# A streaming encoder step: the feed-forward in two phases, with the gate and up projections by a seven-product scheme

## The reference

```python
def causal_dwconv(u, prev, w, b):
    L = u.shape[1]
    full = jnp.concatenate([prev.astype(u.dtype), u], axis=1)
    out = b + sum(full[:, i:i + L] * w[i] for i in range(CONV_W))
    return out, full[:, -(CONV_W - 1):]

def conv_glu(h, prev, w_in, conv_w, conv_b, w_out):
    g, u = jnp.split(h @ w_in, [D_FF], axis=-1)
    gc, new_prev = causal_dwconv(g, prev, conv_w, conv_b)
    return (jax.nn.gelu(gc, approximate=False) * u) @ w_out, new_prev
```

## Time and profile before

| | before |
|---|---|
| median of 3 runs | 2745.13 us |
| profiled execution, first to last instruction | 2742.7 us |
| around that span, if it took the median | 2.4 us |
| TensorE busy | 2688.9 us (98%) |
| VectorE busy | 1199.6 us (44%) |
| ScalarE busy | 902.6 us (33%) |
| GpSimd busy | 799.4 us (29%) |
| DMA | 156.83 MB, mean 57 GB/s |

### The profile page before, as it was taken

The page is one execution under the profiler, slowest core; times in us unless marked ns, Lnnn a source line. Parts: engine busy times, 40 slices in busy tenths (PEclk is TensorE's granted clock), DMA queues, the critical chain, the costliest instruction groups (busy, mean ns, idle before and its releaser), DMA issues.

```text
span 2742.7 us, 41556 instructions
## 1 busy us (share of the span) xinstructions
PE 2688.9 (98%) x17198; PEld 2600.8 (95%) x17198; DVE 1199.6 (44%) x2298; ACT 902.6 (33%) x1617; POOL 799.4 (29%) x452
## 2 busy tenths in 40 slices
PE   8999999999999999999999989999999999999999
PEld 7899999999999999999998988888999999999999
DVE  6634344463333333333625866555633333333324
ACT  7333242451111111112447756444521111111121
POOL 4122221262222222223422223322532222222221
PEclk9999999999999999999999999999999999999999
DMA  3110101011111111111213352212011111111112
GB/s 106 37 39 30 49 20 49 21 46 47 47 47 47 47 47 47 47 47 47 68 43 121 110 215 95 83 53 70 16 47 47 47 47 47 47 47 47 47 47 80
DMA packets 156508, 156.83 MB, mean 57 GB/s; under 512 B 15121, under 2 KB 137631, under 8 KB 156207
## 3 DMA queue, kind: packets, MB, share of 16 engines
q1 hardware_dynamic: 153935, 152.20, 17.5%
q10 hardware_dynamic: 2400, 2.10, 0.3%
HBM read 128.12 MB, written 26.15 MB: 56 GB/s over the span
## 4 chain that ended last, share of the span: by engine, by line
PE 88%; DVE 6%; issue 2%; ACT 2%; DMA 1%; SPq 0%; POOL 0%; DVEq 0%; ACTq 0%; POOLq 0%
PE ps L309 25%; PE ps L310 24%; PE ps L311 24%; PE ps L1933 2%; PE ps L862 1%; PE ps L1917 1%; DVE xT L536 1%; PE ps L849 1%; PE ps L850 1%; PE ps L851 1%; DVE fa L721 1%; PE ps L933 1%; PE ps L918 1%; PE ps L1900 1%; PE ps L1899 1%
## 5 line engine op out<-in xcount | busy, mean ns | idle before, releaser
L309 PE MATMUL ps<-hh,whi 128*128 128x352 f32 x2664 | 864.6, 325 | 0.7 <-DVE hl L443 0.4
L310 PE MATMUL ps<-hl,whi 128*128 128x352 f32 x2664 | 854.8, 321 | 0.0
L311 PE MATMUL ps<-hh,wlo 128*128 128x352 f32 x2664 | 854.5, 321 | 0.0
L274 POOL TENSOR_TENSOR wlo<-wraw,whi 128x2048 fp32r<-128x2048 f32 (+1 forms) x79 | 361.6, 4577 | 652.5 <-ACT whi L267 623.0
L309 PEld LDWEIGHTS ps<-hh,whi 128*128 128x128 f32 x2664 | 500.6, 188 | 3.8 <-issue 1.3
L310 PEld LDWEIGHTS ps<-hl,whi 128*128 128x128 f32 x2664 | 501.4, 188 | 1.1 <-issue 0.2
L311 PEld LDWEIGHTS ps<-hh,wlo 128*128 128x128 f32 x2664 | 499.9, 188 | 0.0
L536 DVE TENSOR_TENSOR xT<-xT,ps 128x352 f32<-128x352 f32 x720 | 372.0, 520 | 262.7 <-PE ps L311 261.4
L267 ACT ACTIVATE whi<-wraw 128x2048 fp32r<-128x2048 f32 x82 | 157.1, 1915 | 578.6 <-DMA wraw<-w_ffn_in 456.7
L309 PE MATMUL ps<-fahi,whi 128*128 128x352 f32 x1056 | 343.5, 325 | 2.5
L311 PE MATMUL ps<-fahi,wlo 128*128 128x352 f32 x1056 | 341.2, 323 | 0.0
(11 more groups left out here) (330 smaller groups left out, 4223.1 us busy)
## 6 DMA issues: line engine op xcount, KB each, us to landing
wraw<-w_ffn_in SPq DMA_DIRECT2D x88, 512.0 KB, 5.0
wraw<-w_ffn_out SPq DMA_DIRECT2D x44, 512.0 KB, 3.9
wraw<-w_gla_in SPq DMA_DIRECT2D x24, 512.0 KB, 4.7
s_k<-kw SPq DMA_DIRECT2D x8, 784.0 KB, 3.3
akraw<-s_k SPq DMA_DIRECT2D x8, 784.0 KB, 4.3
s_v<-vst SPq DMA_DIRECT2D x8, 768.0 KB, 4.3
av<-s_v SPq DMA_DIRECT2D x8, 768.0 KB, 4.1
aqraw<-s_q SPq DMA_DIRECT2D x8, 528.0 KB, 5.7
```

Source lines behind the costliest of these rows:

```text
L274: pool.tensor_tensor(lo[:, 0:cols], raw[:, 0:cols], hi[:, 0:cols].bitcast(F32), ALU.subtract).then_inc(S("w_lo"), 1)
L309: nc.tensor.matmul(out, w[0], x[0], start=start, stop=False)
L310: nc.tensor.matmul(out, w[0], x[1], start=False, stop=False)
L311: return nc.tensor.matmul(out, w[1], x[0], start=False, stop=stop)
```

## The change

The feed-forward of each layer is cut into two phases. Phase one computes all gate and up tiles, phase two all down projections.

Tile f = 0 is computed as before. For the other 21 tiles the pair (gate, up) is one block product: the weights are a 2 x 2 block matrix (gate or up x k 0 to 3 or k 4 to 7), h is a 2 x 2 block matrix (k 0 to 3 or k 4 to 7 x the first or the last 528 tokens). Seven block products take the place of eight. `product` does one in 24 matmuls of 264 columns, into two PSUM banks. Three of the seven need sums of weights (S2, S3, S4, and a fourth in place of the gate-side block), four need sums of activations (T1 to T4, made once a layer in `t_sums`). ScalarE takes partial sums out of PSUM after products 1, 3 and 5 (`snap`), VectorE adds the other products to them (`gate_left`, `the_rest`).

h stays in SBUF as before; its sums T1 to T4 take the room of x and of the activations. So x goes to DRAM (`s_x`) before phase one and comes back at its end, and the hidden activations go to DRAM tile by tile (`s_a`) and come back in phase two, two at a time. VectorE's first operation of the feed-forward waits until x is out (`x_spilled`). The down projection is the same count of matmuls of 352 columns; the first group adds to the x that came back. The loops of SyncE, ScalarE, VectorE and GpSimd over groups are written out.

```diff
@@ -51,9 +51,11 @@
 FF = 2816
 NF = FF // P
 NFG = NF // 2
-NPAIR = (NFG - 1) // 2 - 1
-GW = 2 + SEQ + 2 + DEC
-CW = GW - 2
+NU = NF - 1
...
+            def x_out(j):
+                sp.wait_ge(S("down_added"), 2 + 24 * (b0 - 1) + KD * (j + 1))
+                sp.dma_start(A["s_x"][:, :, tc(j)], xT[:, :, tc(j)]).then_inc(S("x_spilled"), 16)
...
+        def product(bank, w, x, more=False):
+
+            for s in range(2):
+                for k in range(HK):
+                    w_, x_ = [v[:, k * P:(k + 1) * P] for v in w], [v(k, s) for v in x]
+                    out, first = ps[:, bank + s, 0:HH], k == 0 and not more
+                    nc.tensor.matmul(out, w_[0], x_[0], start=first, stop=False, skip_group_check=True)
+                    nc.tensor.matmul(out, w_[0], x_[1], start=False, stop=False, skip_group_check=True)
+                    last = nc.tensor.matmul(out, w_[1], x_[0], start=False, stop=(k == HK - 1), skip_group_check=True)
+            return last
+
...
+            pe.wait_ge(S("w_lo"), c[1] + 1)
+            if u:
+                pe.wait_ge(S("snap"), nth("snap", 3 * u))
+            product(U_SUM, w_in(0), x_part(0, 0)).then_inc(S("prod"), 1)
+            if f == 1:
+                pe.wait_ge(S("gate_taken"), 2 * layer + 1)
+            else:
+                pe.wait_ge(S("summed"), nth("summed", 4 * u - 1))
+            product(U_DOWN, w_in(1), x_part(HK, 0)).then_inc(S("prod"), 1)
+            pe.wait_ge(S("s_lo"), nth("s_lo", 3 * u + 1))
+            pe.wait_ge(S("snap"), nth("snap", 3 * u + 1))
+            if f == 1:
+                pe.wait_ge(S("t_lo_dve"), nth("t_lo_dve", 2 * layer + 1))
+            product(U_SUM, w_extra(0), t_part("T2"), True).then_inc(S("prod"), 1)
+            pe.wait_ge(S("s_lo"), nth("s_lo", 3 * u + 2))
+            if f == 1:
+                pe.wait_ge(S("gate_taken"), 2 * layer + 2)
+                pe.wait_ge(S("t_lo"), nth("t_lo", 2 * layer + 1))
+            else:
+                pe.wait_ge(S("summed"), nth("summed", 4 * u))
+            product(U_SIDE, w_in(2), t_part("T1")).then_inc(S("prod"), 1)
+            pe.wait_ge(S("s_lo"), nth("s_lo", 3 * u + 3))
+            pe.wait_ge(S("snap"), nth("snap", 3 * u + 2))
+            if f == 1:
+                pe.wait_ge(S("t_lo"), nth("t_lo", 2 * layer + 2))
+            product(U_SUM, w_extra(1), t_part("T3"), True).then_inc(S("prod"), 1)
+            pe.wait_ge(S("summed"), nth("summed", 4 * u + 1))
+            if f == 1:
+                pe.wait_ge(S("t_lo_dve"), nth("t_lo_dve", 2 * layer + 2))
+            product(U_DOWN, w_in(3), t_part("T4")).then_inc(S("prod"), 1)
+            pe.wait_ge(S("summed"), nth("summed", 4 * u + 2))
+            product(U_SIDE, w_extra(2), x_part(HK, TH), True).then_inc(S("prod"), 1)
...
+        def pe_ffn(pe, layer, c0, b0, n, m):
+
+            pe_ffn_start(pe, chunk(c0), n, m, b0)
+            for f in range(1, NF):
+                pe_unit_ffn(pe, layer, chunk(c0 + f), f)
+            pe_down_first(pe, layer, chunk(c0 + NF), 24 * b0)
+            for g in range(1, NFG - 1):
+                pe_down_ffn(pe, layer, chunk(c0 + NF + g), 24 * (b0 + g), g)
+            pe_down_ffn(pe, layer, chunk(c0 + NF + NFG - 1), 24 * (b0 + NFG - 1), NFG - 1,
+                        after=y_after(pe) if layer else sums_after(pe, 2), banks=C_BANKS if layer else END_BANKS)
...
+            w_hi_in(1)
+            w_hi_sums(1)
+            t_high(1, "T1")
+            gate_first()
+            t_high(3, "T2")
+            snap(1, 0)
+            t_high(2, "T3")
+            up_first()
+            t_high(4, "T4")
+            for f in range(1, NF):
+                if f > 1:
+                    snap(f, 0)
+                    gelu(f - 1)
+                if 1 < f < NF - 1:
+                    w_hi_in(f + 1)
+                if f == NF - 1:
+                    act_split(act, chunk(c0 + NF), WC)
+                snap(f, 1)
+                if f == 1:
+                    gelu(0)
+                    w_hi_in(2)
+                if f < NF - 1:
+                    w_hi_sums(f + 1)
+                else:
+                    a_high(0)
+                snap(f, 2)
...
+            def s_sums(f):
...
+                    dve.wait_ge(S("prod"), nth("prod", 7 * (u - 1)))
+                dve.tensor_tensor(s3, w[0], w[2], ALU.subtract).then_inc(S("s_sum"), 1)
+                dve.wait_ge(S("s_sum"), nth("s_sum", 4 * u + 1))
+                dve.tensor_tensor(w[2], w[2], w[3], ALU.add).then_inc(S("s_sum"), 1)
+                dve.wait_ge(S("s_sum"), nth("s_sum", 4 * u + 2))
+                dve.tensor_tensor(s2, w[2], w[0], ALU.subtract).then_inc(S("s_sum"), 1)
+                dve.wait_ge(S("s_sum"), nth("s_sum", 4 * u + 3))
+                dve.tensor_tensor(s4, w[1], s2, ALU.subtract).then_inc(S("s_sum"), 1)
+
+            def t_sums():
+
+                x11, x21, x12, x22 = [t_raw[n] for n in ("T1", "T4", "T3", "T2")]
+                dve.wait_ge(S("h32"), KD * NCH * (m + 1))
+                dve.wait_ge(S("h_hi"), KD * NCH * (m + 1))
+                dve.wait_ge(S("h_lo"), POOL_LO * NCH * (m + 1))
+                dve.tensor_tensor(x11, x12, x11, ALU.subtract).then_inc(S("t_sum"), 1)
+                dve.wait_ge(S("t_sum"), nth("t_sum", 4 * layer + 1))
+                dve.tensor_tensor(x12, x22, x12, ALU.subtract).then_inc(S("t_sum"), 1)
+                dve.wait_ge(S("t_sum"), nth("t_sum", 4 * layer + 2))
+                dve.tensor_tensor(x22, x22, x11, ALU.subtract).then_inc(S("t_sum"), 1)
+                dve.wait_ge(S("t_sum"), nth("t_sum", 4 * layer + 3))
+                dve.tensor_tensor(x21, x21, x22, ALU.subtract).then_inc(S("t_sum"), 1)
...
+            def gate_left(f):
+
+                u = unit_no(layer, f)
+                v = two_of(fg[f % 2][:, 2:2 + TH])
+                dve.wait_ge(S("snap"), nth("snap", 3 * u + 1))
+                dve.wait_ge(S("prod"), nth("prod", 7 * u + 2))
+                dve.tensor_tensor(v, v, two(U_DOWN), ALU.add).then_inc(S("summed"), 1)
+
+            def the_rest(f):
+
+                u = unit_no(layer, f)
+                left, right = [two_of(a_rows(f)[:, n, :]) for n in range(2)]
+                dve.wait_ge(S("snap"), nth("snap", 3 * u + 3))
+                dve.tensor_tensor(right, left, two(U_SIDE), ALU.add).then_inc(S("summed"), 1)
+                dve.wait_ge(S("prod"), nth("prod", 7 * u + 6))
+                dve.wait_ge(S("summed"), nth("summed", 4 * u + 2))
+                dve.tensor_tensor(left, left, two(U_DOWN), ALU.add).then_inc(S("summed"), 1)
+                dve.wait_ge(S("prod"), nth("prod", 7 * u + 7))
+                v = two_of(fg[f % 2][:, 2 + TH:2 + T])
+                dve.tensor_tensor(v, v, two(U_SIDE), ALU.add).then_inc(S("summed"), 1)
...
+            dve.wait_ge(S("x_spilled"), nth("x_spilled", 16 * NCH * (layer + 1)))
...
+                last = dve.memset(fg[i][:, 0:2], 0.0)
+            last.then_inc(S("row_zeros"), 1)
+            s_sums(1)
+            t_sums()
+            t_low("T2", 2)
+            gate_left(1)
+            conv(0)
+            t_low("T4", 4)
+            s_sums(2)
+            glu(0)
+            the_rest(1)
+            conv(1)
+            for f in range(2, NF):
+                gate_left(f)
+                glu(f - 1)
+                if f + 1 < NF:
+                    s_sums(f + 1)
+                the_rest(f)
+                conv(f)
...
+            def t_low(name, n):
+                pool.wait_ge(S("t_hi"), nth("t_hi", 4 * layer + n))
+                pool.wait_ge(S("t_sum"), nth("t_sum", 4 * layer + 3))
+                pool.tensor_tensor(t_lo[name][:, :, :], t_raw[name], t_hi[name][:, :, :].bitcast(F32),
+                                   ALU.subtract).then_inc(S("t_lo"), 1)
...
+            w_low_in(1)
+            w_low_first(1)
+            w_low_side(1)
+            t_low("T1", 1)
+            w_low_last(1)
+            t_low("T3", 3)
+            for f in range(2, NF):
+                w_low_in(f)
+                w_low_first(f)
+                w_low_side(f)
+                w_low_last(f)
+            for g in range(NFG):
+                pool_split(pool, chunk(c0 + NF + g), WC)
+                a_low(g)
...
```

More of the change, by code:

```diff
@@ new lines, in pe_down_first, with a_part @@
+        def pe_down_first(pe, layer, c, before):
+            slot, n, _, _ = c
+            wv = w_views(slot, 0, 2, D)
+            def a_part(flat, k, j):
+                if j == 1:
+                    return middle(flat, 2 * k * T + TC, T - TC)
+                t0 = 2 * k * T if j == 0 else (2 * k + 1) * T + 2 * TC - TH
+                return flat[:, t0:t0 + TC]
+            pe.wait_ge(S("a_lo"), NFG * layer + 1)
+            pe.wait_ge(S("w_lo"), n + 1)
+            pe.wait_ge(S("snap"), nth("snap", 3 * NU * (layer + 1)))
+            for i in range(KD * NCH):
+                m, j = tile_of(i, False)
+                if i == 4:
+                    pe.wait_ge(S("summed"), nth("summed", 4 * NU * (layer + 1) - 1))
```

(24 more changed lines are left out.)

483 lines of the change are left out of this document (303 added, 180 removed).

## The result

The changed kernel takes 2669.35 us (median of 4 runs, 2667.98 to 2670.43); the kernel before took 2746.05 on the same chip. The ratio is 0.9718, 95% interval 0.9704 to 0.9733. The forecast was 2674, range 2648 to 2702. The profiled execution took 2669.07 us, of which 2667.2 are span. So the time was close, and in part by luck: two of the terms behind it were each some 10 us off, in opposite directions, and a third was 7 off.

What follows compares the result with a forecast made beforehand. TensorE was taken as the bound (busy 98% of the span), time being matmul count times distance. 2745.1 less 100.0 for matmuls, plus 3 for waits, plus 26 for two starts: 2674 us; own range 2658 to 2688, eight in ten 2648 to 2702.

Steps and rivals of the forecast that it cites:

- The matmuls: Gate/up tiles: 168 matmuls of 264 columns at 0.1221 us replace 144 of 352; 20.51 us instead of 22.89, saving 100.0 us.
- waits: Inside a tile: seven products have 12 to 15 waits where the old tile had 3; costs 3 us in all.
- The bare stream: Rival: fixed part per matmul vanishes, 264 columns take 112.5 ns, a tile 18.9 us; 2607 us, chance 0.04.
- Tiles 2 to 21: Later scheme tiles: work between products fits into 20.5 us, so they wait for nothing; otherwise each late microsecond costs 42.
- The start of each layer: Tile 1: T sums and weight sums on VectorE and GpSimd have no cover; TensorE waits 13 us a layer, 26 in two.
- everything in turn: Upper end for a layer's start: VectorE and GpSimd never overlap, product 7 of tile 1 at 633.8 us, 18.1 late.
- the factor 0.79: Layer start: 1.64 us of VectorE and GpSimd work takes 1.29 together; by it product 7 starts at 624.8, 9.1 late.
- The places named: Tile 1: the wait shows first at product 3, for T2's low part, and again at products 5, 6 and 7.
- The turn of phases: Between phases: 8.1 MB come back in 22 us at 363 GB/s, landing at 25 of 32 us; costs nothing.
- keeps its price: Down projection: its 1584 matmuls a layer stay and cost the same as before.
- free starts: Rival: VectorE and GpSimd hardly collide at the layer starts; 2649 us, chance 0.15.
- late transfers: Rival: at the turn, returning x and activations move at 215 GB/s; 2691 us, chance 0.12.

Runs made afterwards that it cites:

- x5: Changed kernel without the T sums and their parts; all 21 scheme tiles multiply quarters of x instead, in as many matmuls: 2632.97 us, ratio 0.9585.
- x8: Changed kernel with VectorE's start reordered, all T low parts and those of tile 1's weights on VectorE, GpSimd idle until tile 2: 2655.12 us, ratio 0.9664.
- x3: Changed kernel with 84 and 26 filler matmuls into an unused bank ahead of products 3 and 7 of tile 1: 2668.55 us, ratio 0.9713.
- x1: Changed kernel where tile 1 of each layer multiplies quarters of x instead of T1 to T4 and waits for no T: 2670.5 us, ratio 0.9722.
- x6: Kernel before, with three PSUM banks instead of two for the down groups between gate/up tiles: 2739.67 against 2747.49 us, ratio 0.9972.
- x10: Changed kernel with both loads of x at the turn issued behind product 6 of the last tile, group 1's activations load behind them: 2678.9 us, ratio 0.9752.

## Why the prediction was right, and where it was not

**The matmuls** (100.0 us, and 3 back for waits: 97). Measured 42 x (22.89 - 20.41) = 104.2. The line between 256 and 352 columns gave 0.1221 us a step and the trace has 0.1215 with all waits in it; what the waits cost is in it and was not measured apart. The term was right in kind, its size 7 us small: 3 for waits and 4 for the step (20.41 us a tile instead of 20.51). The bare stream of 112.5 ns falls.

**Tiles 2 to 21** wait for nothing: 421.00 of 421 us, as stated. (There are 40 such tiles in two layers, not the 42 that the prediction multiplies a late microsecond by; its sum does not use it.)

**The start of each layer** (13 us, 26 in two) is the step that was mis-sized: 38.2 us by the trace, 19.1 a layer, and 36.4 by x5. The prediction had this size as its upper bound: everything in turn gave product 7 at 633.8 us, 18.1 late, and it started at 634.16. I took the factor 0.79 from the earlier trace rows, operations of 0.7 and 0.95 us that met in part, and reasoned that longer ones collide less. Here both engines had work waiting until GpSimd was done at 622.6 us, and then nearly all of GpSimd's work is time that VectorE loses: its queue took 41.2 us from 590.37 to 631.57, of which its own work is some 25 (an estimate from the durations of these operations where GpSimd is idle), so it lost 16 us to GpSimd's 18. x8 shows the cause by taking GpSimd away (9.53 us for four sums instead of 14.6). The rule of the Trainium skill (page "SBUF — State Buffer", Who interferes with whom), by which one waits for the other's whole instruction, would have been the better guide: by it in full the start was 18.1 us late. The trace agrees (4.45 against 2.35 us).

That 633.8 and 634.16 lie so close is partly chance. Product 1 started 1.1 us later than in the sum, VectorE lost 16 us and not 18, and the 1.82 us for ScalarE's copy were not in the sum. Behind product 7's start comes the low clock, 1.0 to 1.3 us a layer by x3, where the prediction had 1.4.

The places named were right (product 3 for T2's low part, then 6 and 7, though not 5), but the order of cause was not: x1 shows that the wait for T2 costs nothing while L997 stands where it stands.

**The turn of phases** (0). Right in that nothing waits there, but with less room: the changed kernel has group 1's last split 1.9 us early (1.8 in layer 1), where the prediction worked out 32 - 25 = 7. Its loads landed some 30 us behind the start of product 1 of tile 21, not 25. Wrong in that "keeps its price" was taken for the down projection. In the kernel before each of 20 down groups lost 0.41 us because its third step waited for the first add, and that stood behind VectorE's product for the tile ahead (8.2 us; x6 wins 7.8 from 18 of them). Two phases remove that. The row for it was in the profile of before, as 8.7 us of idle time of the weight loads of L309, and I had read the windows of 99.8% busy as "nothing else is late".

**The sum with measured terms**: 2745.1 - 104.2 + 36.4 - 8.2 = 2669.1 us; the profiled execution took 2669.07. With 38.2 for the starts it is 2670.9, so the sum holds to some 2 us, and that it meets the time to a tenth is chance. The forecast's 2674 is a gain put 15 us too low and a loss put 10 to 12 us too low, of which 5 remain: that the total came so close is luck, though the kinds of the two large terms were right. Of the rivals, free starts (2649) would have needed the starts to cost nothing, and late transfers did not come, though x10 brings them by issuing x's loads 8.7 and 5.8 us later.
